# Value products of a softmax branch: two heads and both parts in one matmul, in a new order of heads and blocks

## The reference, cut to what matters

```
def masked_softmax(s, mask):
    s = jnp.where(mask, s.astype(jnp.float32), NEG)
    return jax.nn.softmax(s, axis=-1) * mask
...
        p_cmp = masked_softmax(s, cmp_end[None, :] <= tq[:, None])
        o_cmp = jnp.einsum('bghqn,bgnd->bghqd', p_cmp, vcT.astype(jnp.float32))
...
        p_slc = masked_softmax(s, m.reshape(B, G, 1, NSA_QBLK, topk * SLC_BLOCK))
        o_slc = jnp.einsum('bghqm,bgqmd->bghqd', p_slc, ...)
...
        p_win = masked_softmax(s, mw)
        o_win = jnp.einsum('bghqk,bgkd->bghqd', p_win, vwb.astype(jnp.float32))
...
    o = g[..., 0:1] * to_bshd(o_cmp) + g[..., 1:2] * to_bshd(o_slc) + g[..., 2:3] * to_bshd(o_win)
```

## Time and profile before

| | us |
|---|---|
| median of 3 runs | 1502.76 |
| lowest and highest run | 1500.36, 1503.28 |
| the profiled execution, span | 1500.5 |
| PE busy in it | 1452.3 |
| DVE busy in it | 828.7 |
| ACT busy in it | 683.7 |
| softmax stage of this branch, steps 3 to 35 | 262.1 to 355.5 |

### The profile page before, as it was taken

One profiled execution on the slowest core, in us unless ns is written; L12 is line 12 of the kernel. 1 busy time (PEld: TensorE's weight loads), 2 busy tenths in 40 slices (PEclk: granted clock), 3 DMA queues, 4 the chain that ended last, 5 costly groups with the idle time before them and its releaser, 6 DMA issues.

```text
span 1500.5 us, 22048 instructions
## 1 busy us (share of the span) xinstructions
PE 1452.3 (97%) x8524; PEld 1226.9 (82%) x8524; DVE 828.7 (55%) x1455; ACT 683.7 (46%) x1302; POOL 201.9 (13%) x319
## 2 busy tenths in 40 slices
PE   7999999899999999999999999989999999999997
PEld 4887876678988888888998777769988888888996
DVE  6678646776645444432275577574754444422474
ACT  4565536676542222221363556676532232321563
POOL 0000000443310000000130222451300000000221
PEclk9999999999999999999999999999999999999999
DMA  9542440004033333333404211503133333332321
GB/s 365 197 167 85 124 157 10 1 2 169 2 99 98 98 98 98 94 95 94 152 3 167 71 57 43 169 16 99 33 109 98 94 92 96 103 105 92 120 85 56
DMA packets 42148, 146.71 MB, mean 98 GB/s; under 512 B 4673, under 2 KB 7121, under 8 KB 41682
## 3 DMA queue, kind: packets, MB, share of 16 engines
q1 hardware_dynamic: 37986, 128.99, 27.2%
q0 software_dynamic: 3072, 15.71, 2.8%
q10 hardware_dynamic: 1008, 0.89, 0.2%
HBM read 141.39 MB, written 4.19 MB: 97 GB/s over the span
## 4 chain that ended last, share of the span: by engine, by line
PE 84%; DVE 9%; ACT 3%; issue 2%; DMA 1%; POOL 0%; DVEq 0%; SPq 0%; ACTq 0%; POOLq 0%
PE B L285 22%; PE B L287 22%; PE B L286 22%; PE CROW_P L285 3%; PE CROW_P L287 3%; PE CROW_P L286 3%; PE B L1789 2%; PE B L2025 1%; DVE AL L1381 1%; DVE WADA L1143 1%; PE CROW_P L1868 1%; ACT T L622 1%; PE CROW_P L1768 1%; ACT AH L622 1%; DVE WL L1110 1%
## 5 line engine op out<-in xcount | busy, mean ns | idle before, releaser
L285 PE MATMUL B<-UH,WH 128*128 128x512 f32 (+1 forms) x1008 | 374.7, 372 | 4.6 <-DVE WL L1110 3.7
L287 PE MATMUL B<-UH,WL 128*128 128x512 f32 (+1 forms) x1008 | 372.3, 369 | 0.0
L286 PE MATMUL B<-UL,WH 128*128 128x512 f32 (+1 forms) x1008 | 372.3, 369 | 0.0
L622 ACT ACTIVATE WH<-RAW 128x1024 fp32r<-128x1024 f32 x174 | 182.6, 1052 | 120.0 <-DMA RAW<-in_stream 111.6
L285 PEld LDWEIGHTS B<-UH,WH 128*128 128x128 f32 x1008 | 190.4, 189 | 38.0 <-issue 5.0
L286 PEld LDWEIGHTS B<-UL,WH 128*128 128x128 f32 x1008 | 190.3, 189 | 32.0
L287 PEld LDWEIGHTS B<-UH,WL 128*128 128x128 f32 x1008 | 190.2, 189 | 32.0
L1110 DVE TENSOR_TENSOR WL<-RAW,WH 128x1024 fp32r<-128x1024 f32 x94 | 116.0, 1240 | 143.8 <-ACT WH L622 143.7
L1462 DVE TENSOR_TENSOR WL<-RAW,WH 128x1024 fp32r<-128x1024 f32 x80 | 98.0, 1226 | 76.7 <-ACT WH L622 73.9
L622 ACT ACTIVATE T<-B 128x256 f32<-128x256 f32 (+5 forms) x186 | 86.5, 465 | 109.9 <-PE B L287 63.3
L622 ACT ACTIVATE T<-T 128x512 f32<-128x512 f32 (+3 forms) x131 | 68.7, 525 | 130.8 <-DVE T L1466 119.2
(11 more groups left out here) (419 smaller groups left out, 3146.2 us busy)
## 6 DMA issues: line engine op xcount, KB each, us to landing
RAW<-in_stream SPq DMA_DIRECT2D x202, 512.0 KB, 3.7
WADA<-in_w_ada SPq DMA_DIRECT2D x8, 1024.0 KB, 16.7
RAW<-in_stream SPq DMA_DIRECT2D x16, 384.0 KB, 3.5
WADA<-in_w_ada SPq DMA_DIRECT2D x2, 2048.0 KB, 11.5
W<-in_w POOLq DMA_DIRECT2D x2, 2048.0 KB, 12.1
X<-in_x SPq DMA_DIRECT2D x2, 1024.0 KB, 11.0
DECAY<-in_decay POOLq DMA_DIRECT2D x1, 2048.0 KB, 9.6
X<-in_x POOLq DMA_DIRECT2D x2, 1024.0 KB, 8.2
```

Source lines behind the costliest of these rows:

```text
L285: nc.tensor.matmul(out, lh, rh, start=start, stop=False, **kw)
L286: nc.tensor.matmul(out, lh, rl, start=False, stop=False, **kw)
L287: return nc.tensor.matmul(out, ll, rh, start=False, stop=stop, **kw)
L622: return nc.scalar.activation(out, in_, func, **kw)
```

## The change

The two rounds of a kind over heads `j` and `j + 1` now share their products. The order of the rounds becomes, for each two heads: the rounds of 1 and 4 key blocks of kind 0 for both heads, then of kind 1, then those of 2 and 3 key blocks in the same way. By number of key blocks this is 1, 4, 1, 4, 1, 4, 1, 4, 2, 3, 2, 3, 2, 3, 2, 3, twice.

The high and low values lie side by side in one tile `VN`, so that one stationary operand of 128 columns holds both. A value product is two matmuls for each key block and two heads (high weights and low weights, 256 columns each) where it was three for each head (128 columns each). Rows 0 to 63 of the bank collect the high values' part, rows 64 to 127 the low values' part; the second matmul now includes low by low as well. The products are issued by `nsa_values` at steps 6, 7, 10, 11, 14, 15 and so on (the steps with m mod 4 of 2 or 3): at the first for the rounds m-6 and m-4, at the second the next two.

Eight rounds (a "G" in the code) now cover two heads and two blocks of queries. After each G the bank is read in two steps: ScalarE copies rows 0 to 63 (two copies of 64x256 for each group), VectorE adds rows 64 to 127 (two additions for each group, `at_a`), then the gate, high and low parts follow at half width (`at_m`, `at_hi`, `at_lo`, 128x256 each). The bank is free again with `at_a`. The compressed branch's matmul is split in two of half the width.

```
-        NSA_ORDER = ((0, 0), (0, 3), (1, 0), (1, 3), (0, 1), (0, 2), (1, 1), (1, 2))
-        NSA_UNITS = [nsa_unit(h, kind, i) for j in range(4) for kind, i in NSA_ORDER for h in (j, j + 4)]
+        NSA_BLOCKS = ((0, 3), (1, 2))
+        NSA_UNITS = [nsa_unit(h, kind, i) for jj in range(2) for blocks in NSA_BLOCKS for kind in range(2)
+                     for j in (2 * jj, 2 * jj + 1) for i in blocks for h in (j, j + 4)]
...
-                    if m >= 4:
-                        for s in range(2):
...
-                            for b in range(i + 1):
-                                ins = mm3(B[s][0:HD, i * P:(i + 1) * P], *x["v"](b), AH2[:, u % 4, b * P:(b + 1) * P],
-                                          AL2[:, u % 4, b * P:(b + 1) * P], b == 0 and (tag is BAND or (m - 4) % 8 == 0), b == i, skip_group_check=True)
...
+                    values(m)
...
+            def nsa_values(m):
+
+                t, x = divmod(m - 6, 4)
+                if m < 6 or x > 1:
+                    return
+                G, last = t // 2, 4 * t + 2 + x
+                i, (AH_, AL_) = NSA_UNITS[2 * last]["i"], ((AHA, ALA), (AHB, ALB))[x]
+                for g in range(2):
+                    out = B[g][:, 2 * P * x:2 * P * x + 2 * P]
+                    wait(pe, NSA["lo"], 2 * last + g + 1)
+                    if x == 0 and t % 2 == 0:
+                        wait(pe, at_a, 4 * G - 2 + 2 * g)
+                    for b in range(i + 1):
+                        V = VN[:, b, 2 * (t % 2) + g, :, :]
+                        mat(out, V, AH_[:, g, b, :], start=x == 0 and t % 2 == 0 and b == 0, stop=False, skip_group_check=True)
+                        ins = mat(out, V, AL_[:, g, b, :], start=False, stop=t % 2 == 1 and b == i, skip_group_check=True)
...
+            def nsa_behind(m):
+                G = (m - 12) // 8
+                if m >= 12 and m % 8 == 4:
+                    for g in range(2):
+                        low = B[g][HD:P, :].rearrange("p (i j q) -> p i j q", i=2, j=2)
+                        for j in range(2):
+                            tile = group_tokens(T[10 + g][pair_rows(j), :], G)
+                            wait(dve, at_x, 4 * G + 2 * g + j + 1)
+                            at_a.mark(tt(tile, tile, low[:, :, j, :], ALU.add))
+                if m >= 13 and m % 8 == (5 if m < 36 else 4):
+                    for g in range(2):
+                        tile = group_tokens(T[10 + g][:, :], G)
+                        wait(dve, at_a, 4 * G + 2 * g + 2)
+                        at_m.mark(tt(tile, tile, group_tokens(RG[:, 1, G // 2 + 2 * g, :], G), ALU.mult))
```

More of the change, by code:

```diff
@@ L503, in _ @@
             wait(pool, E["gn_g"], 4)
-            wait(pool, at_m, 4)
+            wait(pool, at_m, 8)
             for k in range(2):
@@ L801, in _, with softmax_pairs @@
                     gn_hi((m - 12) // 4)
-            def softmax_pairs(units, tag, ahead):
+            def softmax_pairs(units, tag, ahead, parts, summed):
                 N = len(units) // 2
@@ L812, in softmax_pairs @@
                             wait(act, tag["tr"], u + 1)
-                            wait(act, tag["pv"], u - 3)
-                            tag["hi"].mark(f(AH2[:, u % 4, 0:(i + 1) * P], PT_BANK[s][:, 0:(i + 1) * P], ACT.Copy))
+                            wait(act, tag["pv"], summed(u))
+                            tag["hi"].mark(f(parts(u)[0], by_block(PT_BANK[s][:, 0:(i + 1) * P]), ACT.Copy))
                     if m < N:
@@ L1356, in compressed_softmax, with softmax_pairs @@
                     E["cmp_p"].mark(tt(SCB[:, :, :, :], SCB[:, :, :, :], sm.unsqueeze(3).broadcast_to([P, TT, NH, 32]), ALU.mult))
-            def softmax_pairs(units, tag, ahead):
+            def softmax_pairs(units, tag, ahead, parts, behind=lambda m: None):
                 N = len(units) // 2
@@ L1403, in nsa_ahead @@
                     gn_lo(3)
-                if m in (20, 36):
-                    for s in range(2):
-                        p = m // 36 + 2 * s
-                        wait(dve, at_x, 4 * (m // 36) + 3 + s)
-                        at_m.mark(tt(T[10 + s][:, :], T[10 + s][:, :], RG[:, 1, p, :], ALU.mult))
-                if m in (21, 37):
-                    for s in range(2):
-                        p = m // 37 + 2 * s
-                        wait(dve, at_hi, 2 * (m // 37) + s + 1)
-                        at_lo.mark(tt(UL[:, 4 + p, :], T[10 + s][:, :], UH[:, 4 + p, :], ALU.subtract))
                 if m in (30, 32):
@@ L1837, in transposes, with softmax_pairs @@
                 return ins
-            def softmax_pairs(units, tag, ahead, first):
+            def softmax_pairs(units, tag, ahead, values):
                 N = len(units) // 2
@@ L2110, in band_ahead, with band_values @@
                     heads_stats(SBN, B[7])
+            def band_values(m):
+                for s in range(2):
+                    u = 2 * (m - 4) + s
+                    if u < 0:
+                        return
+                    x = BAND_UNITS[u]
+                    i = x["i"]
+                    band_first(m - 4, s)
+                    wait(pe, BAND["lo"], u + 1)
+                    for b in range(i + 1):
+                        ins = mm3(B[s][0:HD, i * P:(i + 1) * P], *x["v"](b), AH2[:, u % 4, b * P:(b + 1) * P],
+                                  AL2[:, u % 4, b * P:(b + 1) * P], b == 0, b == i, skip_group_check=True)
+                    BAND["pv"].mark(ins)
             def band_first(m, s):
```

101 lines of the change are left out of this document (60 added, 41 removed).

## The result

| | before | after |
|---|---|---|
| median, us | 1502.77 | 1514.55 |
| lowest and highest run | 1500.36, 1503.28 | 1512.84, 1515.31 |
| profiled execution, span | 1500.5 | 1513.3 |
| first scores of the stage (step 0) | 253.76 | 254.53 |
| first bank complete (start of step 12) | 292.35 | 297.56 |

The change makes the kernel slower: ratio 1.0078, 95% interval 1.0063 to 1.0092. That is outside my range of 1499 to 1511, on the side that I had thought the likelier one. All of the 12.8 us of the span is there at the end of the last products; what follows takes 1145.0 us in both. Of the 12.8, 0.8 stands ahead of the stage's first scores, where the change only writes the values' parts to other places, and 12.0 are the stage's own.

A forecast was written before the change was run, and what follows sets the result against it. TensorE was taken as the bound, with a nearly as long ring of transposes, high and low parts behind it. Terms +1.0, -0.1, +0.8, +1.4 and 0 gave +3.1 us on 1502.76: 1505.9 us, range 1499 to 1511.

The forecast's parts named there:

- Part 1: Value products on TensorE: 256-column matmuls start every 0.12 us; TensorE sheds 12.3 us, of which at most 9.2 counts.
- the empty steps: Steps with m mod 4 of 0 or 1, without value products: TensorE waits 1.66 us for low parts in two.
- Part 3: Four-step cycles traced engine by engine: waits in steps without products leave nothing of TensorE's saving; 9.54 against 9.42 us.
- the bursts' loss: Four-step cycle with products gathered in two steps: 1.66 us of TensorE waiting in the two without products.
- the shape's gain: Four-step cycle, value products with the 128-column operand: 1.5 us less work on TensorE.
- the walk: Engine-by-engine timing of four-step cycles from trace prices: 9.54 us with 1 and 4 blocks, 11.7 where additions stand.
- an addition was priced at 0.34 us: VectorE's four 64x256 additions per eight rounds: bounded by 0.28 below and 0.59 above, taken as 0.34 each.
- VectorE becomes the bound: Whole second half of the stage: additions over 0.45 us make VectorE the bound, about 1510 us; chance 0.20.
- the cycle of steps 20 to 27: Eight steps with rounds of 1 and 4 key blocks: 23.3 us against 22.51, +0.8.
- the start: From 283.57 us to the first complete bank: 9.8 against 8.78 us, +1.0; before that 0.
- The last cycle: Steps 28 to 35: weight splitting joins the additions on VectorE, bare rounds follow; 20.5 against 19.08 us, +1.4.
- `at_lo` falls in a burst and costs nothing: Low parts after each eight rounds: run during grouped products, where VectorE has room, cost 0; otherwise 0.67 us.

The follow-up runs named there:

- fill: The changed kernel plus useless 512-column matmuls on TensorE where it stood idle longest, nothing left out; 1510.69 us.
- burst3: The changed kernel with three old 64-row products of 256 columns in the new places, and so without additions; 1509.56 us.
- old_adds: The kernel before plus four 64x256 additions on VectorE at steps 12, 20 and 28, result unused; 1505.77 us.
- order_only: The changed kernel's round order and half-width bank reading, but the old products of the kernel before in every step, no additions; 1503.20 us.
- smooth: The changed kernel with additions, multiplications, high and low parts spread over later steps, and group 1's products and copies moved a step later; 1513.40 us.
- old_adds8: The kernel before plus eight 64x256 additions on VectorE at steps 12, 20 and 28, result unused; 1512.45 us.
- spread: The changed kernel with group 1's additions, the multiplications and the high and low parts a step later, nothing left out; 1513.77 us.
- noadd: The changed kernel without the four additions after each eight rounds, bank rows 64 to 127 left out of the result; 1506.41 us.

## Why the prediction was wrong

**The direction and the mechanism held.** The product matmuls are 0.12 us apart, as Part 1 took from the earlier trace rows. Nothing of the saving survives: the empty steps wait for VectorE's low parts, as Part 3 walked. Part 3 had the bursts' loss and the shape's gain about even. Measured they are 6.4 us lost and 3.2 won, but with the clock down in part of both kernels; at full clock the estimate above has them 1 us apart. The order itself costs nothing that can be measured.

**First failed step: the clock is in no term.** Every price of the walk is one at 2.4 GHz, since the earlier trace rows have clock 1.00 in all stretches. The walk itself gave TensorE 1.66 us of waiting in two empty steps, and 2.2 more (11.7 against 9.54) where the additions stand, and never asked what the clock does then. It falls in each of the three long waits shown above, and at 283.3, in the last of three waits for transposes (0.97, 0.30 and 1.55 us) before 284.35. Keeping TensorE at work instead brings 3.9 us back (fill), and that time, 1510.69, would have been inside the range. A page would have been the warning: the Trainium skill ("TensorE: Matmul & The Clock Gate", section "A second HAM failure mode: psum-queue depth-cycling") describes a kernel in which TensorE idles briefly between groups of matmuls and the clock goes up and down between its two levels. The traces here agree in kind (0.50 behind the long waits of the kernel after, 1.00 through the stage before). The prediction looked at the stage as it was, where TensorE looked full; the waits were still to be made by the change.

**Second: an addition was priced at 0.34 us and takes 0.456.** It is a form of 64 rows, and I had put it between forms of 128 rows, nearer to the lower. The measured duration, 424 ns, is that of the 128x256 forms (416); the rows left out buy nothing, and four additions that don't need each other still follow at 0.456, not at the 0.34 of the low parts' pairs. By 4 x 0.12 that is 0.5 us for each cycle. The rival "VectorE becomes the bound" was said to decide from 0.45 us; the addition is just over it, and the cycle of steps 20 to 27 is over 24 us, as that rival said. Its price, about 1510, fits fill, 1510.69, where most of the clock's part is gone, and is 4.5 us under the measured 1514.55. So the two failed steps together carry the time out of the range: the addition's price moves it within the range, the clock past the end.

**Third: the start.** Before the first bank I had +1.0 us. From the first scores on it is +4.4, and +1.7 with the clock held (fill), so most of this miss is again the clock; another 0.8 of the 5.2 us stands ahead of the first scores, within what kernels alike up to there differ by. The walk began at the burst and passed over the transposes of the compressed branch (L1943, L1911 before), which wait for low parts too. In the kernel before, value products run until 282.8 and the wait ahead of these transposes is 0.77 us; after, the step has no products and TensorE waits 1.55 us there, then runs the transposes and the next scores at 1.2 GHz. The row of the kernel after:

```profile
284.35 1.09 PE L1943 MATMUL CROW_P<-CONST,SCB 128*128 128x128 f32 x4 [1.55 <-DVE ALA L1413]
```

**Fourth: the drain.** The last cycle had +1.4 and has +3.3, and +3.4 in fill, where the clock is down for 3.4 us instead of 6.9. So this is not mainly the clock. Bursts alone give it +1.7 (burst3) and additions alone +1.2 (old_adds), both at full clock. In the trace of the kernel after the last low parts stand behind `at_lo` (358.86, 0.74 us) and the weights' split (359.52, 1.22 us) in VectorE's queue, in steps in which no bunched product is left to cover the wait; TensorE's wait there is 1.09 us:

```profile
361.35 0.87 PE L1912 MATMUL CROW_P<-CONST,T 128*128 128x128 f32 x4 [1.09 <-DVE ALB L1413]
```

I had said that `at_lo` falls in a burst and costs nothing. In the first two cycles it does (309.83 and 333.76), and the next transposes don't wait. In the last it pushes the split into the steps behind the burst. No run takes `at_lo` or the split away, so their share of the 3.3 us is read from the trace, not tested.

By terms, forecast against measured in the profiled execution: ahead of the stage 0 and +0.8; start +1.0 and +4.4; steps 12 to 19, -0.1 and +2.0; 20 to 27, +0.8 and +2.3; 28 to 35, +1.4 and +3.3; projection 0 and 0. In fill the middle two are +0.7 and +1.6, which the addition's true price (+0.5 each) brings close to the forecast. The terms in the middle were sound but for that price, the start was 0.7 too low with the clock held; the clock and the last cycle were wrong.

What stays open: of the 6.2 us that bursts with the old products cost in the profiled executions, 2.3 lie before the first bank, where burst3's clock is down for 6.8 us. The other 3.9 lie in the three cycles at full clock, and burst3 shows there only 2.6 us more of visible waits than order_only (4.6 against 2.0); the rest lies in short waits that TensorE's modelled ends hide, or elsewhere, and wasn't separated. Nor did the runs show when a wait brings the clock down. I also haven't found an order that keeps the wide operand and hides the low parts in the steps without products; smooth shows that the cycle of steps 12 to 19 can come down to 22.25 with all the work in it, but not the ends.

## What to carry to other kernels

Work on the bounding engine that fills another engine's turn-round is not only a cost: before taking or bunching it, walk the steps that are left without it, and where the walk gives waits of a microsecond or two on TensorE, price the products behind them at both levels of the clock. Price an instruction on few rows by the free size of its nearest form, not by its rows. Compare kernels from the first instruction of the changed stage on, not by points of time in the trace: here the stage began up to 5.5 us apart in kernels with the same instructions ahead of it. And when two operands are joined into one wide one, look for a row with that width of the stationary side at the planned number of moving columns: the time of one matmul can nearly double at few columns.

## What the runs showed of the hardware

- Matmuls of 128 moving columns (float32 in reduced form) start 0.06 us apart with 64 stationary columns (load 0.14 us in the trace) and 0.11 apart with 128 (load 0.19). With 256 moving columns and 128 stationary ones it is 0.12.
- TensorE's granted clock fell from 2.4 to 1.2 GHz in or just behind waits of 2.28 and 2.60 us (after), 3.70 and 2.50 us (old_adds8) and 1.37 us (spread), and stayed down for 3.4 to 13.7 us at a time. It stayed up around waits of 1.95 us in old_adds, of 2.50 us before 299.86 in old_adds8, and of 1.37 and 1.68 us in smooth. The length of the single wait doesn't tell which it will be.
- In the same instructions, 3.4 us more at the lower clock made the stretch before the first bank 1.4 to 1.5 us longer (after against noadd and spread) and 0.7 us longer (old_adds8 against before).
- Useless matmuls in such waits made the kernel 3.9 us faster, but where the clock would have stayed up they cost 1.2 to 1.7 us a cycle.
- Additions of 64x256 with one operand in a bank take 424 ns and follow one another at 0.456 us; the 128x256 form of the earlier trace rows takes 416 ns. Here 64 rows cost what 128 rows cost.
